# Attention trunk on one core: the values become the matmul's weights, pairs of query tiles move, 64-wide heads come out feature-major

## The chip, the cores and the metric

One core of a Trainium2 chip runs the whole program. The metric is the device time of one execution in microseconds (us). PE is TensorE, DVE is VectorE, ACT is ScalarE, POOL is GpSimd and SP is SyncE, which here only issues DMAs.

## What is computed

One layer over 1024 frames of width 1024, all in float32:

```
h = rmsnorm(x);  proj = h @ w_in
A: 4 heads, two maps of 64 each, values 128 wide, chunk-causal with a T5 bias; a = p0 - lam*p1; per-head rmsnorm
B: 8 heads of 64, band of own + 8 previous chunks (at most 5 tiles of 128 keys), relative bias
C: 8 heads of 64, causal, score + c_q - c_k from the forget gates
x += (sum_i sigmoid(gate_i) * (o_i @ w_br_i)) @ w_out
x += (silu(gt) * up) @ w_down;  out = rmsnorm(x)
```

## The kernel before

Every product that needs full accuracy is made of float32r halves: a high part (a rounded copy, made by ACT) and a low part (the rest, made by DVE or, for the weights, by POOL), and three passes (high x high, high x low, low x high). The program is four blocks, one after the other: norm, attention, merge, feed-forward. Each engine has its own instruction stream, in the order of the code, and waits on semaphores.

**Attention** is 12 units of two 64-wide maps or heads: units 0 to 3 are branch A (one head each), 4 to 7 branch B, 8 to 11 branch C. The first two branches are loops of two iterations over two units each; the units of C are written out. A unit has 16 steps s, and s stands for query tile i = s // 2 (128 queries) and map or head m = s % 2. Of each step:

- PE `score`: q tile is the weights, up to 8 key tiles move; the scores of map m land in two PSUM banks (m = 0: banks 0 and 1, m = 1: banks 2 and 3). In C one more matmul adds the causal mask on the diagonal tile.
- DVE `read_scores`: adds the bias, takes the row's extreme, writes `probs` (4 buffers). In C also `shift`.
- ACT `exp`, with the row's sum.
- PE `turn_probs`: transposes of the 128x128 tiles into banks 4 and 5, one chunk of up to 4 tiles in each. ACT `chunks_hi` and DVE `chunks_low` take each chunk out as `probs_t_hi` and `probs_t_lo`.
- PE `times_v`: for each key tile, the transposed probabilities are the weights and the values move, 128 columns in B and C (64 high, 64 low), 256 in A; once with the high and once with the low part. ACT `o_low_part` scales the half that came from the low values by 1/rowsum, DVE `o_out_part` scales the other, adds, and writes `heads` (2 buffers).

In A, `mix_maps` on DVE joins the two maps, and there is a transpose and a product only for every second step.

Between these PE makes the next unit's projection: 6 groups g of 512 frames (k, k, q, q, v, v), each in 4 **pieces** of 6 matmuls of 512 columns. `PIECES_AT[s]` says how many pieces step s has; 4 come ahead of step 0. A group's result is taken out of PSUM by `project_out` (ACT, two halves of 64 partitions) and `project_low` (DVE, two halves, for k and q) at the step that `EVAC_AT` names. In all units but 0 every group uses bank 6. The first piece of a group waits until the group before it is out:

```
if part == 0 and not (isinstance(unit, int) and unit == 0):
    pe.wait_ge(proj_out, 6 * unit + g)
```

PE's order in a step is: score(s+2), turn_probs(s), pieces, times_v(s-1). DVE's is: o_out_part(s-2), mix_maps (A), project_low, read_scores(s+2), chunks_low(s), and the reciprocal of the rowsum (B, C). ACT's is: o_low_part(s-2), project_out, chunks_hi(s), exp(s+2), and, at the steps of `SPLIT_AT`, the high part of a weight slab; POOL then makes its low part (`split_lo`, L559), three a unit. SP loads slabs and biases, shifts k between partitions, and stores `heads` to HBM token-major after each unit.

**Merge** goes over the branches in the order B, C, A, and in each over 8 feature tiles q: gate matmuls (2 halves x 24 matmuls of 512 columns), branch matmuls (24), sigmoid on ACT, products on DVE. The heads come back from HBM token-major, so each branch's heads are transposed on PE (L1203, 32 transposes of 128x128), B's all ahead of the first branch matmul, C's and A's one tile for each q through `heads_tile` (`stage`, L1141 for A, L1144 for C). The first gate (q = 0) is made in the last attention unit. Lines to know: L187 to L189 the three passes, L847/L848 score, L876 turn_probs, L895/L897 times_v, L694 to L703 project_low, L730 read_scores, L745 chunks_low, L773 o_out_part.

Of the kernel before, what the change touches and what calls it, by code (L numbers as in the profile page):

```python
# [26 lines left out]
F32 = mybir.dt.float32  # L27
# [5 lines left out]
P = 128  # L33
D = 1024
# [58 lines left out]
UNIT_TURNS = [len(turns_of(b)) for b in range(N_BRANCH)]  # L93
assert all(c % 2 == 0 for c in UNIT_CHUNKS)
V_CHUNKS = 2

# [7 lines left out]
PIECES_AT = [  # L104
# [20 lines left out]
assert all(PIECES_BEFORE + sum(pieces) == 6 * GROUP_PIECES for pieces in PIECES_AT)  # L125


def counts(b, it, du):

    unit = UPB * b + du + 2 * it  # L130
    local = du + 2 * it
    chunks = sum(UNIT_CHUNKS[:b]) * UPB + UNIT_CHUNKS[b] * local
    turns = sum(UNIT_TURNS[:b]) * UPB + UNIT_TURNS[b] * local
    return dict(unit=unit, local=local, step=STEPS * unit, chunks=chunks, turns=turns,
                banks=chunks + V_CHUNKS * unit)


def build(nc, x, norm_mix_g, w_in, b_forget, diff_lambda, diff_subln_g, t5_table, b_rel_table,
# [8 lines left out]
        heads=nc.dram_tensor("heads_scratch", (N_BRANCH, T, BR_W), F32, kind="Internal").ap(),  # L147
# [12 lines left out]

# [32 lines left out]
def block_norm(nc, ps, keep, scratch, x_tiles, norm_mix_g, w_in_k, b_forget, diff_lambda, diff_subln_g,  # L193
               t5_table, b_rel_table, norm_ffn_g, t5_onehot, rel_onehot):
    h_hi, h_lo, ident = keep["h_hi"], keep["h_lo"], keep["ident"]
    with ExitStack() as ctx:
        sb = lambda name, shape, dt=F32: ctx.enter_context(nc.sbuf_tensor(name, shape, dt))
        sem = lambda name: ctx.enter_context(nc.semaphore(name))
        x_all = sb("x_all", [P, TT, D])
# [7 lines left out]
        mask = sb("mask", [P, P])  # L207
# [50 lines left out]
        def _(pool):  # L258
            nc.gpsimd.memset(ident[:, :], 0.0).then_inc(made, 1)
            nc.gpsimd.memset(mask[:, :], 0.0).then_inc(made, 1)  # L260
            nc.gpsimd.memset(ones[:, :], 1.0).then_inc(made, 1)
            pool.wait_ge(made, 3)
# [3 lines left out]
            nc.gpsimd.affine_select(out=mask[:, :], in_=mask[:, :], compare_op=ALU.is_ge, fill=NEG,  # L266
# [1467 lines left out]
```

## Time and profile before

| | |
|---|---|
| median of 3 runs | 2133.78 us (2132.53 to 2134.18) |
| the profiled execution: its time, its span | 2137.23 us, 2135.5 us |
| granted TensorE clock, mean | 0.992 |
| PE busy | 2044.8 us, 96% of the span |
| PE weight loads busy | 1686.9 us, 79% |
| DVE, ACT, POOL busy | 942.5 (44%), 713.5 (33%), 97.6 us (5%) |
| DMA | 133.56 MB, 63 GB/s mean |

A matmul's duration in the trace reaches into the next one's (they are pipelined), so what a matmul costs is read from start to start. A unit of attention is bounded here by the first transpose of its values (L858): units begin at 87.2, 147.8, 208.4, 268.9 (A), 329.5, 396.2, 466.6, 533.3 (B), 600.0, 672.1, 744.1 and 813.1 us (C); the merge begins at 864.4.

### The profile page before, as it was taken

The page shows a single profiled execution, that of the slowest core. Times are in us where ns is not written, and L with a number is a line of the kernel's source. Part 1 is how long each engine was busy: PE and PEld are TensorE (multiplying, and loading weights), DVE is VectorE, ACT ScalarE, POOL GpSimd, SP SyncE. Part 2 cuts the span into 40 slices and gives each one's busy share as a digit, 9 for nine tenths or more (in the row PEclk, how much of TensorE's full clock was granted, in tenths as well). Part 3 has the DMA queues.
Part 4 walks back from the last instruction along what each step waited for, and adds up shares of the span by engine and source line. Part 5 has one row for each costly group of instructions (what it writes and reads, how often), then busy time and mean ns, then how long its engine had stood idle before and what let it go on. Part 6 is the DMA issues. An engine that isn't in the chain of part 4 may idle for free. (4 is left out here: it accounts for less than half of the span.)

```text
span 2135.5 us, 27733 instructions
## 1 busy us (share of the span) xinstructions
PE 2044.8 (96%) x10054; PEld 1686.9 (79%) x10054; DVE 942.5 (44%) x1894; ACT 713.5 (33%) x1374; POOL 97.6 (5%) x59
## 2 busy tenths in 40 slices
PE   7999999989999999899999999999999999999997
PEld 3787878878888888787787887778888888888886
DVE  4356665445555566322533236733432334323326
ACT  5355555545554555221332121321121111111122
POOL 1111111110010000000000000000000000000000
PEclk9999999999999999999999999999999999999999
DMA  7322122212222110312111113111121111211111
GB/s 220 106 63 79 40 71 73 72 34 55 65 79 65 50 51 31 113 44 84 44 44 45 44 49 148 40 39 41 59 59 49 31 43 54 59 49 37 43 50 79
DMA packets 153703, 133.56 MB, mean 63 GB/s; under 512 B 7701, under 2 KB 138901, under 8 KB 151305
## 3 DMA queue, kind: packets, MB, share of 16 engines
q1 hardware_dynamic: 150184, 132.16, 21.0%
q8 instruction: 55, 0.90, 0.2%
q10 hardware_dynamic: 3424, 0.17, 0.1%
q14 instruction: 40, 0.32, 0.1%
HBM read 109.17 MB, written 16.06 MB: 59 GB/s over the span
## 5 line engine op out<-in xcount | busy, mean ns | idle before, releaser
L187 PE MATMUL ps<-h_hi,w_hi 128*128 128x512 f32 x1664 | 670.4, 403 | 33.5 <-DVE k_stack L697 21.1
L189 PE MATMUL ps<-h_hi,w_lo 128*128 128x512 f32 x1664 | 658.1, 396 | 0.0
L188 PE MATMUL ps<-h_lo,w_hi 128*128 128x512 f32 x1664 | 657.5, 395 | 0.0
L187 PEld LDWEIGHTS ps<-h_hi,w_hi 128*128 128x128 f32 x1664 | 313.6, 188 | 111.1 <-DVE k_stack L697 26.3
L189 PEld LDWEIGHTS ps<-h_hi,w_lo 128*128 128x128 f32 x1664 | 313.2, 188 | 74.9
L188 PEld LDWEIGHTS ps<-h_lo,w_hi 128*128 128x128 f32 x1664 | 313.8, 189 | 68.4
L1482 DVE TENSOR_TENSOR residual<-residual,ps 128x512 f32<-128x512 f32 x240 | 162.5, 685 | 117.1 <-PE ps L189 112.1
L895 PE MATMUL ps<-v_split,probs_t_hi 128*128 128x128 f32 (+1 forms) x672 | 157.7, 273 | 3.7 <-DVE heads_out L773 3.5
L897 PE MATMUL ps<-v_split,probs_t_lo 128*128 128x128 f32 (+1 forms) x672 | 160.4, 277 | 0.0
L773 DVE SCALAR_TENSOR_TENSOR heads_out<-ps,rinv,o_low 128x64 f32<-128x64 f32 (+1 forms) x160 | 47.6, 297 | 245.3 <-ACT o_low L635 245.3
L730 DVE CUSTOM_DVE_ANT_0 probs<-ps,bias 128x640 f32<-128x640 f32 (+3 forms) x192 | 138.1, 721 | 23.9 <-PE ps L848 18.3
L895 PEld LDWEIGHTS ps<-v_split,probs_t_hi 128*128 128x128 f32 x672 | 128.1, 191 | 12.4 <-DVE heads_out L773 4.9
L897 PEld LDWEIGHTS ps<-v_split,probs_t_lo 128*128 128x128 f32 x672 | 128.4, 191 | 4.8
L1383 ACT ACTIVATE bias<-ps 128x512 f32<-128x512 f32 x44 | 26.1, 593 | 315.0 <-PE ps L189 314.9
L1473 DVE TENSOR_TENSOR w_lo<-w_raw,w_hi 128x1024 fp32r<-128x1024 f32 x46 | 56.4, 1225 | 161.6 <-ACT w_hi L1375 161.6
L617 ACT ACTIVATE probs<-probs,neg_max 128x640 f32<-128x640 f32 (+7 forms) x128 | 94.2, 736 | 99.9 <-DVE neg_max L730 99.4
L188 PE MATMUL ps<-w_down_lo,act_hi 128*128 128x512 f32 x320 | 124.5, 389 | 0.0
L187 PE MATMUL ps<-w_down_hi,act_hi 128*128 128x512 f32 x320 | 124.5, 389 | 0.0
L189 PE MATMUL ps<-w_down_hi,act_lo 128*128 128x512 f32 x320 | 124.5, 389 | 0.0
L745 DVE TENSOR_TENSOR probs_t_lo<-ps,probs_t_hi 128x384 fp32r<-128x384 f32 (+2 forms) x240 | 119.1, 524 | 9.9 <-ACT probs_t_hi L628 9.9
L559 POOL TENSOR_TENSOR w_lo<-w_raw,w_hi 128x1024 fp32r<-128x1024 f32 (+1 forms) x36 | 88.4, 2456 | 663.6 <-ACT w_hi L582 644.2
L628 ACT ACTIVATE probs_t_hi<-ps 128x384 fp32r<-128x384 f32 (+2 forms) x240 | 103.4, 466 | 25.9 <-PE ps L876 23.3
(191 smaller groups left out, 2462.1 us busy)
## 6 DMA issues: line engine op xcount, KB each, us to landing
w_raw<-in_w_in SPq DMA_DIRECT2D x60, 512.0 KB, 5.4
w_raw<-in_w_gate_up SPq DMA_DIRECT2D x44, 512.0 KB, 3.7
k_stack<-k_stack SPq DMA_DIRECT2D x24, 512.0 KB, 6.4
w_raw<-in_w_down SPq DMA_DIRECT2D x22, 512.0 KB, 3.5
heads_scratch<-heads_out SPq DMA_DIRECT2D x12, 512.0 KB, 3.2
bias<-heads_scratch SPq DMA_DIRECT2D x20, 256.0 KB, 4.7
x_all<-in_x SPq DMA_DIRECT2D x8, 512.0 KB, 10.1
bias<-bias_a_scratch SPq DMA_DIRECT2D x4, 1024.0 KB, 7.6
```

The costliest lines, as they stand in the source:

```text
L187: nc.tensor.matmul(out, w_hi, x_hi, start=first, stop=False)
L188: nc.tensor.matmul(out, w_hi, x_lo, start=False, stop=False)
L189: return nc.tensor.matmul(out, w_lo, x_hi, start=False, stop=last)
L559: nc.gpsimd.tensor_tensor(w_lo[part], w_raw[part], w_hi[part].bitcast(F32), ALU.subtract).then_inc(w_split, 1)
L617: nc.scalar.activation(probs[:, s % 4, 0:n], probs[:, s % 4, 0:n], ACT.Exp, scale=-1.0, bias=(shift if b == 2 else neg_max)[:, s % 4:s % 4 ...
L628: nc.scalar.activation(pt_hi[:, lc % 4, 0:size * P], turn_bank[lc % 2][:, 0:size * P], ACT.Copy).then_inc(turned_hi, 1)
L730: nc.vector.tensor_tensor_reduce(out=probs[:, s % 4, 0:n], in0=scores[m][:, 0:n], in1=window, scale=-1.0, scalar=3.0e38, op0=ALU.add, op1= ...
L745: nc.vector.tensor_tensor(pt_lo[:, lc % 4, 0:size * P], turn_bank[lc % 2][:, 0:size * P], pt_hi[:, lc % 4, 0:size * P].bitcast(F32), ALU.s ...
L895: nc.tensor.matmul(pv_bank[:, 0:width], pt_hi[:, lc % 4, x * P:(x + 1) * P], v, start=tile == 0, stop=False)
L897: last = nc.tensor.matmul(pv_bank[:, 0:width], pt_lo[:, lc % 4, x * P:(x + 1) * P], v, start=False, stop=tile == n - 1)
L1473: nc.vector.tensor_tensor(w_lo[kind], w_raw[:, raw, :], w_hi[kind].bitcast(F32), ALU.subtract).then_inc(w_split, 1)
L1482: nc.vector.tensor_tensor(res[:, t, cols], res[:, t, cols], bank(ps, 4 + o % 4), ALU.add).then_inc(added, 1)
```

## The change

In B and C the operands of `times_v` are swapped: the values (64 high and 64 low columns) are the weights, and the transposed probabilities of **two** query tiles, 256 columns, move. The result is feature-major: partitions 0 to 63 and 64 to 127 hold the products of the high and low values, 256 queries wide, in one half of bank 7. Key tiles that only one of the two query tiles sees move 128 columns.

- The steps of B and C are ordered so that a pair of tiles of one head is complete after two steps of each: `place_of` gives (0,0) (1,0) (0,1) (1,1) (2,0) ... for s = 0, 1, 2, 3, 4 ...; score banks go by s % 2.
- A query's rowsum now lies along the free axis of the product, so 1/rowsum is multiplied into the probabilities before they are transposed: `scale_probs`, a DVE TENSOR_SCALAR over the row for each of the 16 steps; `turn_probs` waits for it. Three buffers of probabilities in B and C.
- `o_low_part` and `o_out_part` become one ACT copy and one DVE add of 64x256 for each of 8 groups a unit.
- Scores of more than 4 key tiles are cut in two equal halves, not in 512 and the rest.
- Projection groups 0 and 1 use banks 3 and 1, the others bank 6; one schedule for all branches: pieces earlier, evacuations and weight splits at other steps. The wait quoted above stays.
- `heads` has one buffer, written 3 steps in after the store before it has landed; B's and C's heads are stored feature-major, one contiguous tile a unit. SP issues two slab loads ahead of the store.
- Merge: the heads of B and C are loaded feature-major and split straight from SBUF (`part_high` on ACT, DVE subtract), with no transposes and no staging; A keeps both, and is loaded by one DMA. The weights of gate q = 1 are loaded in the last unit, and its first half is computed ahead of the first branch matmul.
- The causal mask is made at the start of the attention block by POOL and DVE, not in the norm block; `ident` is read from `ident_r`.

```diff
+def place_of(branch, s):
+    if branch == 0:
+        return divmod(s, 2)
+    return 2 * (s // 4) + s % 2, s % 4 // 2
+def halves_of(n):
+    return (1, n * P) if n <= 4 else (2, n * P // 2)
-PIECES_AT = [ [0,2,2,0,2,2,0,2,2,0,2,2,0,1,2,0,1], ... ]
-EVAC_AT = [ {0: 0, 3: 1, 6: 2, 9: 3, 12: 4, 17: 5}, ... ]
-SPLIT_AT = [ {1: 1, 7: 2, 13: 3}, ... ]
+PIECES_AT = [2, 2, 2, 2, 0, 2, 2, 0, 2, 2, 0, 1, 1, 1, 1, 0, 0]
+EVAC_AT = {0: 0, 2: 1, 4: 2, 7: 3, 10: 4, 16: 5}
+SPLIT_AT = {0: 1, 5: 2, 10: 3}
...
-            return bank(ps, (0, 1, 2, 3, 5, 6)[g] if isinstance(unit, int) and unit == 0 else 6)
+            if isinstance(unit, int) and unit in (0, UNITS):
+                return bank(ps, (0, 1, 2, 3, 5, 6)[g] if unit == 0 else 6)
+            return bank(ps, (3, 1, 6, 6, 6, 6)[g])
...
+            def scale_probs(b, c, s):
+                turns = STEPS * (c["unit"] - UPB) + (s + 1)
+                row = probs_of(b, s)[:, 0:tiles_of(b, place_of(b, s)[0])[1] * P]
                 dve.wait_ge(probs_ready, c["step"] + (s + 1))
                 nc.vector.reciprocal(rinv[:, s % 4:s % 4 + 1], rowsum[:, s % 4:s % 4 + 1]).then_inc(rinv_ready, 1)
+                dve.wait_ge(rinv_ready, UPB * UNIT_OUTS + turns)
+                nc.vector.tensor_scalar(row, row, rinv[:, s % 4:s % 4 + 1], None, ALU.mult).then_inc(scaled, 1)
+            def o_out_bc(c, g):
+                near = slice((g % 2) * HD, (g % 2 + 1) * HD)
+                if g == 0:
+                    heads_room(c)
+                dve.wait_ge(o_low_ready, c["outs"] + (g + 1))
+                nc.vector.tensor_tensor(heads[near, g // 2 * 2 * P:(g // 2 + 1) * 2 * P], pv_half(g)[near, :],
+                                        o_low[near, :], ALU.add).then_inc(o_out, 1)
# DVE, one step
-                    if s - 2 in turns:
-                        o_out_part(b, c, s - 2)
+                    if b > 0 and s >= 3 and s % 2 == 1:
+                        o_out_bc(c, (s - 3) // 2)
...
                     if s + 2 < STEPS:
                         read_scores(b, c, s + 2)
+                    if b > 0 and s + 1 < STEPS:
+                        scale_probs(b, c, s + 1)
                     if s in turns:
                         chunks_low(b, c, s)
-                    if b > 0 and s < STEPS:
-                        invert(c, s)
# PE
+                    pe.wait_ge(scaled, STEPS * (c["unit"] - UPB) + (s + 1))
+            def times_v_bc(b, c, g):
+                i, m = 2 * (g // 2), g % 2
+                first, n = keys_of(b, g)
+                if g >= 2:
+                    pe.wait_ge(o_out, c["outs"] + (g - 1))
...
+                pe.wait_ge(turned_out, c["banks"] + (V_CHUNKS + chunks_through(b, 2 * g + 1)))
+                both = [k for k in range(n) if first + k <= i and first + k >= tiles_of(b, i + 1)[0]]
+                one = [k for k in range(n) if k not in both]
+                for k in both + one:
+                    lo = 0 if first + k <= i else P
+                    hi = 2 * P if first + k >= tiles_of(b, i + 1)[0] else P
+                    v = v_st[:, c["par"], first + k, m * P:(m + 1) * P]
+                    nc.tensor.matmul(pv_half(g)[:, lo:hi], v, ptb_hi[:, m, k, lo:hi], start=k == both[0], stop=False)
+                    last = nc.tensor.matmul(pv_half(g)[:, lo:hi], v, ptb_lo[:, m, k, lo:hi], start=False, stop=k == (both + one)[-1])
+                last.then_inc(pv_group, 1)
# merge, PE
             def tile_body(b, nt, q):
-                if b and isinstance(nt, int) and nt == 0:
-                    turn(b, TURNS - 1)
+                if b == N_BRANCH - 1 and isinstance(nt, int) and nt == 0:
+                    turn(TURNS - 1)
                 if isinstance(q, int) and q == 0:
                     pe.sem_inc(gate_ready, 2)
+                    gate(1, [0])
+                elif isinstance(q, int) and q == 1:
+                    gate(1, [1])
...
-                if isinstance(q, int) and q == 0:
-                    for t in range(TURNS):
-                        turn(0, t)
-                if b < N_BRANCH - 1 and not isinstance(nt, int):
-                    turn(b + 1, nt - 1)
+                if b == N_BRANCH - 2 and not (isinstance(nt, int) and nt == 0):
+                    turn(nt - 1)
```

## Rows read from the trace of the kernel before

**Rows 1.** Stretches of five units: us, busy PE PEld DVE ACT POOL, PEclk, DMA, GB/s.

```profile
87.20:147.80 60.60, 56.68 (x310) 48.01 (x309) 36.86 (x86) 30.86 (x67) 8.18 (x4) 1.00 0.18 46
...
329.50:396.20 66.70, 63.56 (x382) 54.89 (x381) 32.99 (x98) 35.10 (x87) 7.59 (x5) 1.00 0.22 59
396.20:466.60 70.40, 65.05 (x382) 56.09 (x381) 33.01 (x98) 35.10 (x87) 7.59 (x5) 0.98 0.25 71
...
672.10:744.10 72.00, 69.49 (x434) 61.07 (x433) 39.48 (x114) 37.81 (x87) 7.22 (x3) 1.00 0.21 60
...
813.10:864.40 51.30, 46.75 (x330) 42.52 (x330) 33.52 (x104) 30.81 (x77) 1.28 (x1) 1.00 0.10 32
```

**Rows 2.** Timeline of PE in an A unit: start, length, engine, line, out<-in.

```profile
104.69 0.40 PE L189 MATMUL ps<-h_hi,w_lo 128*128 128x512 f32 x1
104.92 0.28 PE L895 MATMUL ps<-v_split,probs_t_hi 128*128 128x256 f32 x1
105.04 0.28 PE L897 MATMUL ps<-v_split,probs_t_lo 128*128 128x256 f32 x1
```

**Rows 3.** Timeline of PE in a C unit, times_v.

```profile
700.94 0.27 PE L895 MATMUL ps<-v_split,probs_t_hi 128*128 128x128 f32 x1
701.05 0.27 PE L897 MATMUL ps<-v_split,probs_t_lo 128*128 128x128 f32 x1
```

**Rows 4.** Timeline, all engines: projection group 0 of unit 1 is taken out.

```profile
90.65 0.39 PE L189 MATMUL ps<-h_hi,w_lo 128*128 128x512 f32 x1
...
91.08 0.59 ACT L593 ACTIVATE k_stack<-ps 64x512 fp32r<-64x512 f32 x1 [2.13 <-PE ps L189]
...
91.70 0.68 DVE L694 TENSOR_TENSOR k_stack<-ps,k_stack 64x512 fp32r<-64x512 f32 x1 [1.15 <-ACT k_stack L593]
...
93.15 0.50 PE L187 MATMUL ps<-h_hi,w_hi 128*128 128x512 f32 x1 [1.51 <-DVE k_stack L697]
```

**Rows 5.** Timeline of DVE in a C unit: step with 6 key tiles.

```profile
709.05 0.96 DVE L730 CUSTOM_DVE_ANT_0 probs<-ps,bias 128x768 f32<-128x768 f32 x1
...
710.24 0.88 DVE L745 TENSOR_TENSOR probs_t_lo<-ps,probs_t_hi 128x384 fp32r<-128x384 f32 x2
711.03 0.15 DVE L750 RECIPROCAL rinv<-rowsum 128x1 f32<-128x1 f32 x1
```

**Rows 6.** Groups by line and shape: count, busy us, mean ns.

```profile
L351 DVE TENSOR_SCALAR x_all<-x_all,rstd 128x1024 f32<-128x1024 f32 x8 | 5.5, 749 | 0.1
...
L745 DVE TENSOR_TENSOR probs_t_lo<-ps,probs_t_hi 128x128 fp32r<-128x128 f32 x20 | 5.8, 288 | 3.4 <-ACT probs_t_hi L628 3.4
```

**Rows 7.** Timeline: a POOL split alone; DVE and POOL late in an A unit.

```profile
76.25 2.39 POOL L559 TENSOR_TENSOR w_lo<-w_raw,w_hi 128x1024 fp32r<-128x1024 f32 x1 [4.09 <-ACT w_hi L582]
...
137.60 1.28 DVE L762 SCALAR_TENSOR_TENSOR probs<-probs,ratio 128x1024 f32<-128x1024 f32 x1
...
138.15 2.99 POOL L559 TENSOR_TENSOR w_lo<-w_raw,w_hi 128x1024 fp32r<-128x1024 f32 x1 [18.96 <-ACT w_hi L582]
```

**Rows 8.** Timeline of PE: where the second iteration of B's loop begins.

```profile
461.75 0.47 PE L847 MATMUL ps<-k_stack,q_stack 128*128 128x128 f32 x1 [2.73 <-issue]
```

**Rows 9.** Timeline: end of attention and start of the merge.

```profile
862.47 0.27 PE L897 MATMUL ps<-v_split,probs_t_lo 128*128 128x128 f32 x1
...
864.46 3.56 PE L1203 MATMUL ps<-ident,bias 128*128 128x128 f32 x16 [1.71 <-SPq L1011]
...
879.45 0.50 PE L187 MATMUL ps<-h_hi,w_hi 128*128 128x512 f32 x1 [1.38 <-DVE w_lo L1102]
```

**Rows 10.** Timeline of PE in the merge, branches C and A.

```profile
1000.68 0.66 PE L1203 MATMUL ps<-ident,heads_tile 128*128 128x128 f32 x4 [1.29 <-DVE heads_tile L1144]
...
1146.25 0.66 PE L1203 MATMUL ps<-ident,heads_tile 128*128 128x128 f32 x4 [2.29 <-DVE heads_tile L1141]
```

**Rows 11.** Busy time and granted clock by stretch, behind two long waits.

```profile
462.00:466.00 4.00, 4.00 (x14) 3.34 (x15) 0.60 (x4) 0.88 (x4) 0.00 (x0) 0.62 1.00 313
...
1147.00:1151.00 4.00, 4.00 (x12) 3.15 (x11) 1.35 (x2) 1.15 (x2) 0.00 (x0) 0.59 0.15 45
```

More of the change, by code:

```diff
@@ L87, in chunks_through @@
 def chunks_through(branch, s):
-    return sum(len(chunks_of(branch, x // 2)) for x in turns_of(branch) if x <= s)
+    return sum(len(chunks_of(branch, place_of(branch, x)[0])) for x in turns_of(branch) if x <= s)
+def halves_of(n):
+    return (1, n * P) if n <= 4 else (2, n * P // 2)
 UNIT_CHUNKS = [chunks_through(b, STEPS - 1) for b in range(N_BRANCH)]
-UNIT_TURNS = [len(turns_of(b)) for b in range(N_BRANCH)]
+UNIT_OUTS = 8
 assert all(c % 2 == 0 for c in UNIT_CHUNKS)
@@ L124 @@
 assert sum(LAST_PIECES_AT) == 2 * GROUP_PIECES
-assert all(PIECES_BEFORE + sum(pieces) == 6 * GROUP_PIECES for pieces in PIECES_AT)
+assert PIECES_BEFORE + sum(PIECES_AT) == 6 * GROUP_PIECES
 def counts(b, it, du):
@@ L132, in counts @@
     chunks = sum(UNIT_CHUNKS[:b]) * UPB + UNIT_CHUNKS[b] * local
-    turns = sum(UNIT_TURNS[:b]) * UPB + UNIT_TURNS[b] * local
-    return dict(unit=unit, local=local, step=STEPS * unit, chunks=chunks, turns=turns,
+    return dict(unit=unit, local=local, step=STEPS * unit, chunks=chunks, outs=UNIT_OUTS * unit,
                 banks=chunks + V_CHUNKS * unit)
@@ new lines, in chunks_hi, with o_low_a, o_low_bc @@
+                    tile += size
+            def o_low_a(c, i):
+                act.wait_ge(pv_chunk, c["chunks"] + chunks_through(0, 2 * i + 1))
+                act.wait_ge(rinv_ready, c["outs"] + (i + 1))
+                nc.scalar.activation(o_low[:, i % 2 * P:(i % 2 + 1) * P], pv_bank[:, P:2 * P], ACT.Copy,
+                                     scale=rinv[:, 2 * (i % 2):2 * (i % 2) + 1]).then_inc(o_low_ready, 1)
+            def o_low_bc(c, g):
+                m = g % 2
+                near, far = slice(m * HD, (m + 1) * HD), slice((1 - m) * HD, (2 - m) * HD)
+                act.wait_ge(pv_group, GROUPS * (c["unit"] - UPB) + (g + 1))
+                nc.scalar.activation(o_low[near, :], pv_half(g)[far, :], ACT.Copy).then_inc(o_low_ready, 1)
@@ L924, in unit_body @@
                     if s + 2 < STEPS:
-                        score(b, c, s + 2)
+                        score(b, c, s + 2, last)
                     if s in turns:
@@ L982, in over_tiles @@
             body(0, KT * b)
+            if b == 0:
+                body(1, 1)
             end = KT - 1 if b == N_BRANCH - 1 else KT
-            with eng.Fori(1, end) as nt:
+            with eng.Fori(2 if b == 0 else 1, end) as nt:
                 body(nt, nt + KT * b)
@@ L987, in over_tiles, with flat @@
                 body(KT - 1, LAST)
+        def flat(parts):
+            return parts.rearrange("p k t -> p (k t)")
         def turn_view(t):
@@ L1204, in turn, with gate @@
                 last.then_inc(turned, 1)
+            def gate(q, halves=(0, 1)):
+                pe.wait_ge(g_split, q + 1)
+                for half in halves:
+                    cols = slice(half * HALF, (half + 1) * HALF)
+                    for k in range(KT):
+                        last = three_passes(nc, bank(ps, half), g_hi[:, k, :], g_lo[:, k, :],
+                                            h_hi[:, k, cols], h_lo[:, k, cols], k == 0, k == KT - 1)
+                    last.then_inc(gate_ready, 1)
@@ L1219, in tile_body @@
-                if isinstance(q, int) and q == 0:
-                    for t in range(TURNS):
-                        turn(0, t)
-                if b < N_BRANCH - 1 and not isinstance(nt, int):
-                    turn(b + 1, nt - 1)
+                    gate(1, [0])
+                elif isinstance(q, int) and q == 1:
+                    gate(1, [1])
+                else:
+                    gate(q)
+                if b == N_BRANCH - 2 and not (isinstance(nt, int) and nt == 0):
+                    turn(nt - 1)
```

426 lines of the change are left out of this document (233 added, 193 removed), and 6 rows, old and new, of tables (EVAC_AT, PIECES_AT).

## The prediction

> **What bounds the kernel now.** I read the page first: PE is busy for 96% of the span and no other engine for more than 44% (DVE), so time goes where PE's instructions and PE's waits go. The view by stretches then shows the units [rows 1]: an A unit lasts 60.6 us with PE busy 56.7, a B unit 66.7 with 63.6, a C unit 72.0 with 69.5. The reader is to see two things there. PE idles only 3.9, 3.1 and 2.5 us a unit, so there is little waiting to win; and DVE is busy for 37, 33 and 39.5 us of these, which a step-by-step dependence on DVE could turn into waits. Last the timeline of PE: start to start, a 512-column matmul costs 0.23 us, a 256-column one 0.12 [rows 2], a 128-column one with weights of its own 0.11 [rows 3]. So halving the columns below 256 saves nothing, and a product of 256 columns costs hardly more than one of 128.
>
> **What PE loses in work.** A C unit has 36 key tiles for each of 2 heads (1+...+8), two matmuls each: 144 x 0.111 = 16.0 us. After: pairs of query tiles see 2, 4, 6, 8 key tiles, of which one each is seen by one query tile alone: 32 x 2 x 0.12 + 8 x 2 x 0.111 = 9.4. A B unit goes from 60 tiles (13.3 us) to 24 of 256 and 12 of 128 columns (8.4). So C -6.5, B -4.9. The even cut of five-tile scores (512 + 128 becomes 320 + 320) gives another 0.3 in B and 0.1 in C by columns. Over 8 units -47 us, if PE never waited more than now.
>
> **What the new schedule makes PE wait for.** The wait in `piece` stays, so other banks don't help: group g+1 starts when group g is out, and that takes 2.27 us from the end of the pass (90.88 to 93.15: two ACT halves and two DVE halves) [rows 4]. I counted a unit through in the code's order with these pitches, PE against DVE; each wait below runs from the pitch's end, some 0.2 us more than the row's idle time (1.68 against 1.51 in rows 4), so the units above have 4.7, 4.1 and 3.3 of them.
>
> - A units, PE: before, two scores and a transpose stood between groups 0 and 1, and the count gives the 1.7 of rows 4; now one score does: 2.0. Group 2 follows group 1 in the very next step: 1.9 for 1.6. Group 3 waits 0.55 where it did not, group 4 0.85 for 0.55; the wait of the next unit's first group (0.8) goes, since group 5 ends earlier. The piece that lay between the last transposes and the last product is gone: ACT and DVE need a chunk first, 0.9. Together 6.2 for 4.7: +1.5 a unit, **A +6**.
> - B and C units, the same two waits: 1.9 and 1.75, for 1.6 before.
> - DVE in B and C: each step gets a TENSOR_SCALAR over the row. One of 1024 columns takes 0.75 us and a DVE instruction of 128 columns 0.29 [rows 6]; I take 0.28 + 0.067 per tile, and 0.2 for the reciprocal, whose end it waits for (its pitch alone is 0.07). 16 of them are about 10 us a unit, less 1.3 for half as many, wider output adds. DVE is then busy 43 to 48 us: not the bound by its sum. But it is in order: at s = 4 it stands waiting to take out group 2 and only then reads score 6 and scales step 5, which PE wants next. Group 2 out 2.27 after its end, read 0.8, scale 0.55: 3.6 us, in which PE has two scores, three transposes and a product, 1.8: **wait 1.9**. At s = 7 the chain is longer: product of group g = 2, ACT's copy, DVE's add, two halves of projection group 3, the read of six tiles (1.19 with `shift` [rows 5]), the scale 0.7: 5.35 us after the last piece, against 2.9 of PE work: **wait 2.5**. Later steps balance to within 0.6 in C.
> - The end of a unit: the product now waits for all of its chunks, with no piece ahead: 1.5.
> - What goes: all other waits of before, 2.5 in B and 1.7 in C (behind the first one).
>
> So B: 1.9 + 1.75 + 1.9 + 2.5 + 1.5 = 9.6 for 4.1, +5.5, less 5.2 of work: +0.3. C: 9.6 + 0.6 = 10.2 for 3.3, +6.9, less 6.6: +0.3.
>
> [...] The trace shows the two excluding each other: a POOL split alone takes 2.39 us, the one that began 0.55 us into a DVE operation on two SBUF rows took 2.99, longer by just what DVE had left [rows 7]. Whether DVE's new scaling waits for a split in the same way no row shows. Bounds: nothing, or a whole split for each of the three a unit, 7 us in B and C alike, 56 in all. Where the splits fall (s = 0, 5, 10) DVE has slack in the first two; at s = 10 it has not, and the scale is asked for 0.9 (B) or 0.3 (C) before the split ends. I take 1.2 and 0.3: B +1.5, C +0.6; four B units **+6**, three C units **+2**.
> [...]
>
> **The other terms.** The second iteration of B's loop begins with 2.73 us of PE idle on "issue" [rows 8], in which all engines stand, and then a halved clock: that unit lasts 70.4 for 66.7 [rows 1]. PE's body shrinks from 2 x 382 to 2 x 334 matmuls, near the 2 x 310 of A's loop, which shows no such wait; I take 2.5 of the 3.7: **-2.5** (0 to -3.7). The last unit has 8 pieces and few waits of projection: its work falls by 6.6; its start is serial through DVE (reads, values' low parts, scale) and costs 3 more: counted through 47.5 for 50.5, **-3**. POOL makes the mask ahead of the first split: **+0.5**.
>
> **Merge.** Before, the last product starts at 862.47 and the first gate after it at 879.45, so that gate q = 1 ends at 890.5 (48 x 0.23 on), 28.0 us later [rows 9]; in between stand 32 transposes and 24 matmuls. After: end of block 1.9 as now, ACT's and DVE's split of the gate weights 2.4, half a gate 5.5 with 1.8 for a clock that has fallen behind 4.3 us of waiting, 24 branch matmuls 5.5 (their heads are split meanwhile), the other half 5.5: 22.7. **-5.3.** C's 32 transposes (3.7 with their transitions) and their wait of 1.29 [rows 10] go: **-5.0.** A's are as before. Together -10.5; bounds -6 (if the 4 us of late heads' DMA shows) and -13.
>
> **Clock.** [...] I take one: **+1.5** (0, or +22 if each wait of 1.9 and 2.5 brings one).
>
> **Sum.** +6 (A) +6 (B) +2 (C) -2.5 -3 +0.5 -10.5 +1.5 = 0 on the profiled execution's own 2137.2 us (span 2135.5 and 1.7 around it). That execution is 3.4 above the median of the runs, so the median stays at 2134.
>
> **The rivals.**
> - *PE stays the bound* (faster). If DVE's order costs nothing at s = 5 and s = 8, because scores are read earlier than I count, 4.4 us a unit return in 7 units, and the clock's 1.5: -32, 2102. For it: DVE is busy only two thirds of a B unit. Against it: the two chains consist of instructions whose lengths are all in the rows. In part it can hold: at half, 2118.
> - *The port decides* (slower). A scale that meets a split stands up to 2.4 us, with read, chunk and PE's transposes behind it; at 1.2 us mean on three splits in 7 units that is 25 us, of which I have 6 in the sum; if two thirds reach PE, 17 for my 6: +11, 2145. From about 0.6 us more exposed a unit (4.3 over 7 units) it decides for slower. For it: the exclusion that rows 7 show. Against it: only one scale in five is due during a split.
> - *The clock falls often* (slower): in each of the 7 units with a wait of 2.5, +11 for my 1.5: 2144. With the port, 2154.
> - *The swap does nothing for PE*, the 256-column moves costing twice 0.11: then -47 is gone, 2178; rows 2 exclude it for the same shape, operands only exchanged.
>
> **How the numbers follow.** Forecast, gains eaten by waits, within 2123 to 2143: 0.5. PE the bound, wholly or in part: 0.22. Port: 0.15. Clock: 0.12. The last: 0.01. 2134 us is that of the likeliest; 8 in 10 reach from 2111 to 2149. A difference under 0.2% (4.3 us) is about what a measurement of this kernel can't tell from none; the forecast's own range lies on both sides of it. Faster: 0.16 of its 0.5 and 0.21 of PE's, 0.37. Slower: 0.09 of it, 0.23 of port and clock, and the last, 0.33. Same: 0.30.
>
> **What would show it.** L895/L897's successors in B and C: 304 pairs of matmuls for 528, 0.12 apart. PE's waits in B and C units: on DVE k_stack twice 1.5 to 1.8 us, on the DVE scaling at the 6th and 9th step, 2 to 2.5 us. PE idle 9 to 10 us in a B unit and a C unit, their lengths within 2 us of 66.7 and 72.0; A units 62. The gate of q = 1 ending 23 us behind the last product. A PEclk under 1.00 in some B and C units. A scale lasting much over 0.75 us, or DVE idle ahead of one during a POOL split, would show the port. Wrong it would be if B and C units come out 4 us shorter than now, or 4 longer.

## The result, and the profile after

The changed kernel takes 2156.2 us (median of 4 runs, 2153.4 to 2158.4) beside 2134.0 (4 runs, 2132.5 to 2135.0): 1.010 times the time before, 95% interval 1.009 to 1.012. It is slower by 22 us, where no change was forecast and 2149 us was the upper end of the range. The profiled execution has a span of 2154.3 us, 18.8 more than before.

The view by stretches shows five units that answer to [rows 1]:

```profile
86.00:150.30 64.30, 56.91 (x309) 47.94 (x308) 36.86 (x86) 31.04 (x67) 7.47 (x4) 1.00 0.19 48
150.30:217.70 67.40, 59.97 (x310) 50.59 (x308) 36.87 (x86) 32.26 (x68) 7.43 (x4) 0.95 0.23 64
...
350.70:419.20 68.50, 57.90 (x333) 49.40 (x332) 40.34 (x106) 34.79 (x79) 7.59 (x5) 1.00 0.22 58
...
710.40:789.40 79.00, 67.29 (x370) 57.83 (x369) 47.09 (x122) 37.52 (x79) 7.16 (x3) 0.94 0.19 54
864.40:916.50 52.10, 42.72 (x267) 36.81 (x267) 41.80 (x114) 29.40 (x68) 1.27 (x1) 0.97 0.08 31
```

An A unit, whose products are those of before, lasts 64.3 or 67.4 us for 60.6; the B unit 68.5 for 66.7; the C unit 79.0 for 72.0. PE has fewer instructions in B and C (333 and 370 for 382 and 434), and in the B unit PE is busy for 57.9 us instead of 63.6; what is lost is idle time and, in the units with a clock of 0.94 and 0.95, length of the instructions themselves.

The view of waits, PE in the attention block (what waited, for whom: us in total, times, longest). Before, the largest was `k_stack` with 21.1 us in 15 times, and nothing else was over 5.2:

```profile
PE ps L182 <- DVE k_stack L745: 37.4, 22, 1.9
PE ps L956 <- DVE probs_bc L813: 36.3, 21, 3.2
PE ps L956 <- DVE probs_tb_lo L801: 15.3, 17, 1.4
PE ps L993 <- DVE probs_tb_lo L801: 12.0, 8, 1.7
PE ps L972 <- DVE probs_ta_lo L798: 8.2, 8, 1.1
PE ps L182 <- DVE q_stack L751: 4.3, 8, 0.7
PE ps L956 <- DVE probs_a L825: 2.3, 4, 0.6
```

The first row is the evacuation wait, two in each of 11 units; the second the wait for a scaled row, 21 times in eight units. The next three are waits for low parts, mostly at the ends of units, where pieces used to lie.

What a wait brings beside its own length is in the timeline of PE in a C unit, step 6 to step 9:

```profile
655.36 0.22 PE L930 MATMUL ps<-causal_r,ident_r 128*128 128x128 f32 x1
657.46 0.66 PE L956 MATMUL ps<-ident_r,probs_bc 128*128 128x128 f32 x4 [1.88 <-DVE probs_bc L813]
657.87 0.48 PE L182 MATMUL ps<-h_hi,w_hi 128*128 128x512 f32 x1
658.19 0.39 PE L183 MATMUL ps<-h_lo,w_hi 128*128 128x512 f32 x1
658.42 0.53 PE L184 MATMUL ps<-h_hi,w_lo 128*128 128x512 f32 x1
658.75 0.63 PE L182 MATMUL ps<-h_hi,w_hi 128*128 128x512 f32 x1
659.18 0.63 PE L183 MATMUL ps<-h_lo,w_hi 128*128 128x512 f32 x1
...
661.31 0.63 PE L182 MATMUL ps<-h_hi,w_hi 128*128 128x512 f32 x1
661.74 0.48 PE L183 MATMUL ps<-h_lo,w_hi 128*128 128x512 f32 x1
662.06 0.40 PE L184 MATMUL ps<-h_hi,w_lo 128*128 128x512 f32 x1
...
671.57 0.55 PE L956 MATMUL ps<-ident_r,probs_bc 128*128 128x128 f32 x3 [2.58 <-DVE probs_bc L813]
```

Behind 1.88 us of idle time the passes start 0.43 us apart instead of 0.23, from 658.75 to 661.74, and the granted clock of 657 to 661 is 0.69; from 658.9 to 661.5 it is 0.50. So it stands at half for some eight passes, 1.6 us lost. In attention the trace holds 18 such drops, before 1: five in A, four in B, eight in the three C units of this length, one in the last.

The start of the merge (timeline of PE, answering to [rows 9]; last product, first gate, first pass behind the gate):

```profile
916.54 0.28 PE L994 MATMUL ps<-probs_tb_lo,v_split 128*128 128x128 f32 x1
921.51 0.80 PE L182 MATMUL ps<-h_hi,w_hi 128*128 128x512 f32 x1 [4.70 <-DVE w_lo L1223]
...
939.49 0.39 PE L182 MATMUL ps<-o_hi,w_hi 128*128 128x512 f32 x1
```

The gate of q = 1 ends 22.95 us behind the last product (939.49 less 916.54); 28.2 before, where the first instruction behind it starts at 890.70.

By stages the spans differ so. Attention, from the first transpose of values to the last product: 775.3 before, 830.5 after. Merge, to the first addition of the residual: 426.5 and 406.6. Output projection and norm: 94.0 and 90.9. The rest, the feed-forward block, whose code is the same: 752.5 and 740.3. The last number had no place in the forecast, and the first experiments are about it.

### The profile page after: what moved, and what is told of

It is laid out like the page before. It is cut to its first block and busy times, and to the rows that moved or that the text cites. A ratio compares the mean times of both kernels' runs of the same rounds, so it can differ in the third digit from the quotient of the medians.

```text
span 2154.3 us, 26265 instructions
## 1 busy us (share of the span) xinstructions
PE 1988.8 (92%) x9542; PEld 1647.9 (76%) x9542; DVE 999.7 (46%) x1950; ACT 710.8 (33%) x1310; POOL 94.5 (4%) x59
## 5 line engine op out<-in xcount | busy, mean ns | idle before, releaser
L182 PE MATMUL ps<-h_hi,w_hi 128*128 128x512 f32 x1664 | 674.3, 405 | 51.2 <-DVE k_stack L745 37.4
L184 PE MATMUL ps<-h_hi,w_lo 128*128 128x512 f32 x1664 | 658.9, 396 | 0.0
L184 PEld LDWEIGHTS ps<-h_hi,w_lo 128*128 128x128 f32 x1664 | 318.7, 192 | 69.5
L183 PEld LDWEIGHTS ps<-h_lo,w_hi 128*128 128x128 f32 x1664 | 319.6, 192 | 62.0
L956 PE MATMUL ps<-ident_r,probs_bc 128*128 128x128 f32 x528 | 85.2, 285 | 51.9 <-DVE probs_bc L813 36.3
L780 DVE CUSTOM_DVE_ANT_0 probs_bc<-ps,bias 128x640 f32<-128x640 f32 (+7 forms) x128 | 90.0, 703 | 53.5 <-PE ps L930 24.2
L956 PEld LDWEIGHTS ps<-ident_r,probs_bc 128*128 128x128 f32 x528 | 60.1, 143 | 66.4 <-DVE probs_bc L813 40.8
L1607 DVE TENSOR_TENSOR bias<-ps,bias 128x512 f32<-128x512 f32 x44 | 30.4, 691 | 167.2 <-PE ps L184 167.2
L665 ACT ACTIVATE probs_tb_hi<-ps 128x384 fp32r<-128x384 f32 (+2 forms) x192 | 82.6, 463 | 74.0 <-PE ps L956 72.6
L927 PE MATMUL ps<-k_stack,q_stack 128*128 128x320 f32 (+5 forms) x288 | 98.3, 345 | 0.0
L928 PE MATMUL ps<-k_stack,q_stack 128*128 128x320 f32 (+5 forms) x288 | 95.5, 335 | 0.0
L1504 ACT ACTIVATE act_hi<-bias 128x512 fp32r<-128x512 f32 x44 | 27.8, 632 | 202.9 <-DVE bias L1607 202.9
L801 DVE TENSOR_TENSOR probs_tb_lo<-ps,probs_tb_hi 128x384 fp32r<-128x384 f32 (+2 forms) x192 | 93.8, 516 | 2.1 <-ACT probs_tb_hi L665 1.7
```

The lines of the kernel that those rows point to most:

```text
L182: nc.tensor.matmul(out, w_hi, x_hi, start=first, stop=False)
L183: nc.tensor.matmul(out, w_hi, x_lo, start=False, stop=False)
L184: return nc.tensor.matmul(out, w_lo, x_hi, start=False, stop=last)
L665: nc.scalar.activation(turned_place(ptb_hi, b, i, m, tile, size), turn_bank[lc % 2][:, 0:size * P].rearrange("p (t q) -> p t q", q=P), ACT ...
L780: nc.vector.tensor_tensor_reduce(out=row_view(probs_of(b, s)[:, 0:n * P], n), in0=scores_view(s, n), in1=row_view(window, n), scale=-1.0, ...
L801: nc.vector.tensor_tensor(turned_place(ptb_lo, b, i, m, tile, size), turn_bank[lc % 2][:, 0:size * P].rearrange("p (t q) -> p t q", q=P), ...
```

## The experiments

Twelve kernels, three groups. Where a median is compared, that of the kernel before is 2135 to 2137 us beside these runs, and that of the changed kernel 2156.2. The changed kernel was measured once, beside 2134.0, so differences from it carry up to 3 us of drift.

**1. Where do buffers lie?** The passes over `h_hi` and `h_lo` had been 233 ns apart before and were 227 after. The change dropped one buffer and put the small ones ahead of `h_hi`. (No trace shows an address. What each run differs in is the order and the sizes in which its kernel declares the buffers.)

*place*, the kernel before with that order:

```diff
         keep = dict(
-            h_hi=sb("h_hi", [P, KT, T], F32R), h_lo=sb("h_lo", [P, KT, T], F32R),
-            ident=sb("ident", [P, P]), ident_r=sb("ident_r", [P, P], F32R),
-            causal_r=sb("causal_r", [P, P], F32R),
+            ident_r=sb("ident_r", [P, P], F32R),
...
+            h_hi=sb("h_hi", [P, KT, T], F32R), h_lo=sb("h_lo", [P, KT, T], F32R),
+            ident=sb("ident", [P, P]), causal_r=sb("causal_r", [P, P], F32R),
```

> [...] No instruction differs but in its addresses. Theory (the address of the moving operand sets the pitch of a 512-column matmul): the 4,944 passes over h_hi and h_lo go from a mean of 233.2 ns to 227.4, the up-projection's stage is 12 us shorter, and the whole 29 us: 2105 us. Rival (the shorter pitch after came from something else in the changed program): no change, 2134.

Measured: 2109.7 us, 0.987 of before (0.986 to 0.989). *unplace*, the changed kernel with `h_hi` and `h_lo` moved ahead of the small buffers:

> [...] Address theory: 2156 + 29 = 2185 us, with the pitch at 233 ns again, and a little less in attention, where part of it is hidden by waits: 2178 to 2185. Rival: 2156.

Measured: 2182.2 us, 1.022 of before (1.020 to 1.023). So 26 to 27 us of the changed kernel's time are a gift of the order of the buffers, in either kernel, and the change itself costs 46.

What about the order counts? *pad128* puts 128 bytes (`pad=sb("pad", [P, 32])`) ahead of `h_hi` in the kernel before:

> [...] If the address is not it at all: 2137.

Measured: 2136.5 us, 1.000 (0.999 to 1.001). No pitch changed: 233.2 ns over `h_hi` and `h_lo` in the feed-forward block, 226.9 in the last projection. So the same 128 bytes ahead of the moving operand and of the weights do nothing, to the passes at 233 ns or to those at 227. What is left is the distance between the two. By the author's estimate (worked out in the last section) it is an odd multiple of 128 bytes where passes are 233 ns apart and an even one where they are 227 apart. *padw* has the same line ahead of `bias`, so that 128 bytes more stand between `h_lo` and the weights; *place_padw* is *place* with that line:

> [...] In the slow programs so far (before, unplace, pad128) the moving operand and the weights of a pass lie an odd multiple of 128 bytes apart, in the fast ones (place, the changed kernel, and act_hi with w_down_hi everywhere) an even one. Distance theory: the pitch goes to 227 ns, 2137 - 27 = 2110 us. [...]

> [...] Distance theory: the pitch goes back to 233 ns, 2137 us. Rival (h_hi's address alone): 2110, as place.

Measured: padw 2112.3 us, 0.990 (0.988 to 0.992); place_padw 2137.4, 1.001 (1.000 to 1.002). What stands between the two decides, and not the place of one of them alone: with `h_hi` ahead of the small buffers and with `h_hi` behind them, the same 128 bytes ahead of the weights turn 233.2 ns into 226.7 and 226.7 into 233.2. From the timelines of PE in the feed-forward block, first and last pass of a row of passes: before, 50 passes apart,

```profile
1499.80 0.40 PE L187 MATMUL ps<-h_hi,w_hi 128*128 128x512 f32 x1
...
1511.46 0.40 PE L189 MATMUL ps<-h_hi,w_lo 128*128 128x512 f32 x1
```

padw, 39 passes apart,

```profile
1499.83 0.39 PE L190 MATMUL ps<-h_hi,w_lo 128*128 128x512 f32 x1
...
1508.67 0.39 PE L190 MATMUL ps<-h_hi,w_lo 128*128 128x512 f32 x1
```

and place_padw, 50 passes apart:

```profile
1499.69 0.40 PE L188 MATMUL ps<-h_hi,w_hi 128*128 128x512 f32 x1
...
1511.36 0.40 PE L190 MATMUL ps<-h_hi,w_lo 128*128 128x512 f32 x1
```

11.66 / 50 = 0.2332, 8.84 / 39 = 0.2267, 11.67 / 50 = 0.2334 us. A matmul's own length hardly shows it (0.39 or 0.40); only start to start does.

**2. Which waits, and whose?** *sched* gives the changed kernel the three schedules of before:

```diff
-PIECES_AT = [2, 2, 2, 2, 0, 2, 2, 0, 2, 2, 0, 1, 1, 1, 1, 0, 0]
-EVAC_AT = {0: 0, 2: 1, 4: 2, 7: 3, 10: 4, 16: 5}
-SPLIT_AT = {0: 1, 5: 2, 10: 3}
+PIECES_AT = [0, 2, 2, 0, 2, 2, 0, 2, 2, 0, 2, 2, 0, 1, 2, 0, 1]
+EVAC_AT = {0: 0, 3: 1, 6: 2, 9: 3, 12: 4, 17: 5}
+SPLIT_AT = {1: 1, 7: 2, 13: 3}
```

> The changed kernel with the schedule of before: the steps at which pieces are computed, taken out and split are before's three lists; banks, scaling and the wider products stay. Theory (the bunched pieces cause the evacuation waits, and the halved clock follows them): A units return from 66 to 61.5 us, B and C units lose 3 and 5 us, the clock drops fewer than 8 times in attention for 18: 2156 - 18 - 12 - 15 = 2111 us. Rival (the scaling on DVE causes the waits of B and C): only A returns, 2138 us, and B and C units keep 70 and 78 us.

Measured: 2124.2 us, 0.995 of before (0.993 to 0.996), 32 below the changed kernel. All four A units last 60.0 or 60.1 us, as in *place*; B falls by 2.4 us in all, the three C units by 7.8. Of the 36.6 us between the two profiled executions, 24.5, two thirds, are thus A's, where the product was not changed at all; both theories had A returning, while B and C gave back less than the first had, and nine drops are left in attention where it had fewer than eight. The wait for scaled rows has even grown:

```profile
PE ps L956 <- DVE probs_bc L813: 49.5, 26, 2.9
PE ps L956 <- DVE probs_tb_lo L801: 27.6, 17, 2.7
PE ps L182 <- DVE k_stack L745: 11.7, 8, 1.5
```

*noscale* cuts the scaling's length, not its place in DVE's order (rows beyond their first 8 columns stay unscaled):

```diff
-                nc.vector.tensor_scalar(row, row, rinv[:, s % 4:s % 4 + 1], None, ALU.mult).then_inc(scaled, 1)
+                nc.vector.tensor_scalar(row[:, 0:8], row[:, 0:8], rinv[:, s % 4:s % 4 + 1], None, ALU.mult).then_inc(scaled, 1)
```

> The changed kernel with the scaling of a row cut to its first 8 columns, so DVE keeps the instruction, its waits and its signal, and loses its length (the rows stay unscaled). Theory of the forecast (the scale is the last of DVE's chain ahead of PE's transposes): the waits of 1.9 and 2.5 us at the 6th and 9th step fall to 1.3 and 1.7, the end of the unit by 0.7, 1.9 us a unit and with them half of the drops of the clock: 2156 - 13 - 8 = 2135. Rival (evacuations and reads of DVE alone make these waits): 2150 or above.

Measured: 2134.3 us, 22 below the changed kernel, as expected in sum (2135), though not in its parts. The wait for the scaled row goes from 36.3 us only to 31.0; at the 9th step of a C unit it is 2.26 us for 2.58, shorter by just what that scaling lost (0.55 to 0.23). The rest of the 22 is in low-part waits (15.3 to 8.6) and six drops of the clock fewer. So these waits are made by what DVE has queued ahead of the scaling more than by the scaling. (Scalings that meet a split on POOL did not get shorter, up to 1.3 us for 8 columns; more on this at the end.) The timeline of DVE in the changed kernel, ahead of the 2.58 above, shows that queue:

```profile
667.54 0.42 DVE L846 TENSOR_TENSOR heads_out<-ps,o_low 64x256 f32<-64x256 f32 x1 [2.20 <-ACT o_low L682]
668.16 0.68 DVE L748 SCALAR_TENSOR_TENSOR q_stack<-ps,q_stack 64x512 fp32r<-64x512 f32 x1 [0.20 <-ACT q_stack L630]
668.86 0.69 DVE L751 SCALAR_TENSOR_TENSOR q_stack<-ps,q_stack 64x512 fp32r<-64x512 f32 x1
669.58 0.96 DVE L780 CUSTOM_DVE_ANT_0 probs_bc<-ps,bias 128x768 f32<-128x768 f32 x1
...
670.96 0.55 DVE L813 TENSOR_SCALAR probs_bc<-probs_bc,rinv 128x640 f32<-128x640 f32 x1
```

*loose* takes the evacuation wait away where banks allow it:

```diff
-                    pe.wait_ge(proj_out, 6 * unit + g)
+                    pe.wait_ge(proj_out, 6 * unit + (g if g > 2 else 0))
```

> The changed kernel with the wait ahead of a projection group cut to what its bank needs: groups 1 and 2 stand in banks of their own, so they wait only for group 5 of the unit before, as group 0 does, and no longer for groups 0 and 1. Theory (these two waits, 2.0 and 1.9 us in every unit, and the halved clock behind them are what A's units lost): A units go from 66.2 to 61 us (-4 of waits, -1.5 of clock), B and C units lose half of that, since there the row's scaling waits next: 2156 - 20 - 2.5 x 7 = 2118. Rival (groups leave no faster than DVE and ACT take them out, so group 3 inherits the waits): 2145 or above.

Measured: 2100.7 us, 0.984 of before (0.982 to 0.985), 55 below the changed kernel, a far larger gain than in either expectation. The list of PE's waits is that of the changed kernel with its first row gone (scaled rows 36.1, low parts 15.4, 12.0 and 8.1): 37.4 us of waits went and next to nothing took their place (1.1 us for a weight split), and drops in attention fell from 18 to 7. 37.4 + 11 x 1.6 = 55. A units last 60.4 to 60.7.

*fill* leaves the waits and covers part of them with matmuls whose product is thrown away:

```diff
+                if part == 0 and g in (1, 2) and not (isinstance(unit, int) and unit in (0, UNITS)):
+                    for _ in range(4):
+                        nc.tensor.matmul(proj_bank(unit, g), keep["ident_r"][:, :], h_hi[:, 0, 0:HALF], start=True, stop=True)
                 if part == 0 and not (isinstance(unit, int) and unit == 0):
...
+                    if s in (5, 8):
+                        pe.wait_ge(turned_out, c["banks"] + (V_CHUNKS + done - 1))
+                        for _ in range(4):
+                            nc.tensor.matmul(turn_bank[done % 2], keep["ident_r"][:, :], h_hi[:, 0, 0:HALF], start=True, stop=True)
                     pe.wait_ge(scaled, STEPS * (c["unit"] - UPB) + (s + 1))
```

> The changed kernel with four 512-column matmuls of no use (their product is overwritten) ahead of each of four waits: those for groups 1 and 2 in every unit, and those for the scaled row at the 6th and 9th step of B and C. They last 0.9 us, less than each wait. Theory (a good part of the loss is the halved clock, 18 drops between 86 and 917 us at some 1.7 us each): at least 14 of the 18 go, the waits themselves stay: 2156 - 24 = 2132. Rival (the drops lie mostly in other waits, or filling only adds work): 2156 to 2165.

Measured: 2133.0 us, 0.999 of before (0.998 to 1.000), 23 below the changed kernel, with 3 drops in attention for 18. 23.2 / 15 = 1.5 us a drop. A kernel that computes 152 matmuls more is faster by 23 us; what waits for DVE is otherwise as it was (low parts 15.2, 12.0 and 8.2 us), so this is the price of the clock.

**3. Can both be had?** *sched_late* is *sched* with PE's pieces ahead of its transposes in B and C:

```diff
+                    if b > 0:
+                        next_pieces(pieces_at[s])
                     if s in turns:
                         turn_probs(b, c, s)
-                    next_pieces(pieces_at[s])
+                    if b == 0:
+                        next_pieces(pieces_at[s])
```

> The run sched (changed kernel, schedule of before) with PE's order changed in B and C alone: in each step the pieces of projection come ahead of the transposes of the row. Its turns wait 3.0, 1.3, 2.8 and 1.6 us for the scaled row. Theory (DVE finishes the scaling late in every step by less than two pieces last, 2.8 us, so PE has work to put in front): B units from 69.4 to 66, C units from 75.4 to 71: 2124 - 14 - 13 = 2097. Rival (DVE's order of work is the bound and what PE does first only moves the wait to the next score or group): 2120 to 2130.

Measured: 2083.0 us, 0.975 of before (0.974 to 0.977), 41 below *sched* and 14 below what the first theory gave. B units last 64.4 (one 65.9), C units 68.8 (the last of the three 65.8). PE's largest waits are now these; the wait for scaled rows has gone from 49.5 to 4.1, and a part has come back ahead of the groups:

```profile
PE ps L182 <- DVE k_stack L745: 35.3, 22, 1.9
PE ps L182 <- DVE q_stack L751: 7.9, 11, 1.2
...
PE ps L956 <- DVE probs_bc L813: 4.1, 3, 2.6
```

*best* adds the looser wait to it (`0 if banks_apart else g`, with `banks_apart` for g up to 2, but not in the unit that computes the first gate, whose groups share a bank):

> Changed kernel with the schedule of before, pieces ahead of the transposes in B and C (both as in sched_late), and the wait ahead of groups 1 and 2 cut to what their banks need (as in loose, though not in the unit that computes the first gate). If the two cures act on different waits: A units from 60.0 to 57, B and C units 2 less: 2083 - 12 - 14 = 2057. If what loose removed is only the wait that the bunched schedule made: 2083.

Measured: 2048.5 us, 0.959 of before (0.957 to 0.960), 9 better than expected. The two cures act on different waits: an A unit lasts 57.9 us, a B unit 61.0 to 61.2, a C unit 65.9 (the third 63.0), and one drop is left in attention. By stretches, units 1, 5 and 9:

```profile
144.50:202.40 57.90, 56.12 (x310) 48.01 (x309) 36.78 (x86) 31.80 (x68) 8.16 (x4) 1.00 0.27 75
...
379.20:440.30 61.10, 57.82 (x334) 49.19 (x333) 38.75 (x103) 32.56 (x75) 7.62 (x5) 1.00 0.24 64
...
628.50:694.40 65.90, 62.93 (x370) 54.19 (x369) 49.01 (x122) 36.55 (x79) 7.25 (x3) 1.00 0.23 65
```

*best_dve* also turns DVE's order round in B and C:

```diff
+                    if b > 0 and s + 1 < STEPS:
+                        scale_probs(b, c, s + 1)
                     if project and s in EVAC_AT:
                         project_low(c["unit"] + 1, EVAC_AT[s], 1 - du)
                     if s + 2 < STEPS:
                         read_scores(b, c, s + 2)
-                    if b > 0 and s + 1 < STEPS:
-                        scale_probs(b, c, s + 1)
```

> The run best with DVE's order changed in B and C: the scaling of a row stands ahead of a group's low part and of the next read of scores. If DVE's order is what still delays PE's transposes there: 1 to 1.5 us a unit less, -10 in all. If the read of scores is by now the later of the two: 0 to +10.

Measured: 2060.4 us, 12 above *best*: B and C units 0.4 to 0.8 longer, the last unit 55.6 for 50.5. What comes late with the scaling first is the low part of a projection group: the wait on `q_stack` grows from 1.22 to 1.85 us in a B unit and from 0.49 to 1.37 in a C unit. That is not the read of scores that the second theory named. In the last unit, which takes no group out, the waits for low parts of probabilities grow, most of them 1.2 to 1.7 us each; whether a late read of scores is behind these was not tested.

## Why the prediction was wrong, point by point

The view by stretches of whole branches (A, B, the three C units of full length) of *unplace*, which has the pitch of before (233 ns) and is the fair partner for a forecast that took it as given; its last unit is 52.0:

```profile
86.90:354.30 267.40, 238.53 (x1234) 199.48 (x1233) 147.69 (x344) 125.59 (x269) 29.98 (x17) 0.96 0.22 57
354.30:633.30 279.00, 236.81 (x1332) 200.39 (x1331) 161.34 (x426) 139.01 (x316) 29.94 (x18) 0.99 0.21 57
633.30:867.40 234.10, 198.92 (x1093) 170.16 (x1092) 140.50 (x360) 111.77 (x233) 21.49 (x9) 0.94 0.18 51
```

and of the kernel before:

```profile
87.20:329.50 242.30, 226.58 (x1234) 191.99 (x1233) 147.42 (x344) 124.79 (x269) 32.92 (x17) 1.00 0.23 62
329.50:600.00 270.50, 255.85 (x1523) 220.94 (x1522) 132.41 (x394) 140.50 (x348) 29.95 (x18) 0.99 0.22 59
600.00:813.10 213.10, 205.64 (x1285) 180.88 (x1283) 117.66 (x338) 112.47 (x257) 21.66 (x9) 1.00 0.21 58
```

| term of the sum | forecast | measured, pitch as before |
|---|---|---|
| A's four units | +6 | +25.1 |
| B's four units, with the loop's stall | +3.5 | +8.5 |
| three C units | +2 | +21.0 |
| last unit | -3 | +2.6 |
| mask, start | +0.5 | -0.3 |
| merge | -10.5 | -10.2 |
| clock | +1.5 | 16 drops more (17 for 1), in the rows above |
| output projection | none | -1.3 |
| order of the buffers | none | -26.6 |

The rows come to +45 without the last and +19 with it, which is the difference of the spans.

- **Two steps failed, about equally.** With the pitch of before, attention grew by 57 us (25.1 + 8.5 + 21.0 + 2.6), where the forecast had 8.5 for the new waits less the work saved, and 1.5 for the clock.
- **The clock: "I take one".** No run shows the term, one drop of 1.5 us for all new waits. The rows of before have the granted clock at 0.62 and 0.59 of 4 us behind waits of 2.73 and 2.29 us [rows 8, 10, 11], and at 1.00 in the unit with the wait of 1.51 [rows 1, 4]; they give it for no length between. What the runs showed in its place is 17 drops more in the changed kernel and 16 more in *unplace*, at 1.5 us each by *fill* some 25 us for 1.5. The forecast's own upper bound, "+22 if each wait of 1.9 and 2.5 brings one", is about what came. The waits were there in the forecast; what they would do to the clock was its author's guess. Of the 18 drops of the changed kernel ten stand behind idle times of 1.7 to 1.9 us, four of them in A units, seven behind 2.4 to 3.2, and one behind 1.05. The length does not decide alone: unit 0 has the same waits as unit 1 and no drop, and the first B unit has waits of 1.80 and 2.46 and none. What else decides stays open. The rival "the clock falls often" named the right cause, with one drop in each of 7 units and none in A, and so less than half the price.
- **The size of the waits.** The other 32 us stand against 8.5: the waits at the end of A, B and C units and at the start of the last unit were counted too short, as the next points show.
- **PE's work**, -5.2 in B and -6.6 in C: right. It is best read where the clock keeps still: from *place* to *best*, PE's busy time falls from 254.4 to 231.5 us in B and from 204.5 to 185.9 in three C units, 5.7 and 6.2 a unit (5.3 in B without the one drop that *place* has there). "The swap does nothing" is out.
- **A, +1.5 a unit:** a unit without a drop is 64.3 - 60.0 = 4.3 longer than in *place*. The two evacuation waits (1.87 and 1.76) and the smaller ones came as counted. What was short is the tail, 0.9 for three waits of 0.94, 0.57 and 1.05 in these rows of unit 2; with the 0.2 that the forecast adds to each wait that is some 2.2 of the 2.8 us missing, and the rest stays open:

```profile
273.56 0.38 PE L972 MATMUL ps<-v_split,probs_ta_hi 128*128 128x256 f32 x1 [0.94 <-DVE probs_ta_lo L798]
...
276.06 1.09 PE L956 MATMUL ps<-ident_r,probs_a 128*128 128x128 f32 x8 [0.57 <-DVE probs_a L825]
278.20 0.39 PE L972 MATMUL ps<-v_split,probs_ta_hi 128*128 128x256 f32 x1 [1.05 <-DVE probs_ta_lo L798]
```

  The last pieces hid not one chunk's conversion but the ends of two steps. And "the wait in `piece` stays, so other banks don't help" was true and was the costliest line of the kernel: *loose* shows 55 us behind it.
- **B and C, the waits for the scaled row, 1.9 and 2.5:** measured 1.88 and 2.58 in the C unit above, right. "Later steps within 0.6 in C" was not: low parts at the last steps cost 1.37, 0.84 and 1.66 us in unit 9, for 1.5 + 0.6. A B unit without a drop came out at 68.5 us in the changed kernel and at 68.9 and 69.2 in *unplace*, for a forecast of 68.5 (66.7 + 0.3 + 1.5). That it fits is luck in part: of the port's 1.5 at most 0.6 can have reached PE, and the low parts at its end cost 3.0 (1.31, 0.35 and 1.34) for 1.5. A C unit came out at 79.0, 6.1 above its forecast (72.0 + 0.3 + 0.6): three drops and 1.5 us of waits.
- **PE stays the bound** is refuted for this kernel. It came true in *best*, by other edits than the rival had in mind: PE is busy there for 96% of the span.
- **The port:** no run shows a port. What they show is that a scaling on DVE that meets a split on POOL is held up by it (1.17 us for 0.49), as the forecast assumed; the cost was set too high. Two rows of DVE and one of POOL:

```profile
378.76 2.40 POOL L589 TENSOR_TENSOR w_lo<-w_raw,w_hi 128x1024 fp32r<-128x1024 f32 x1 [17.37 <-ACT w_hi L616]
```

```profile
380.27 1.17 DVE L813 TENSOR_SCALAR probs_bc<-probs_bc,rinv 128x512 f32<-128x512 f32 x1
...
393.62 0.55 DVE L813 TENSOR_SCALAR probs_bc<-probs_bc,rinv 128x640 f32<-128x640 f32 x1
```

  A scaling of 640 columns alone takes 0.55 us, one of 512 that meets a split 1.17; nine of 128 are longer by more than 0.6 and add some 6 us to DVE in all: two in each B unit, one in the last unit, none in the three C units between. The first of a B unit does not reach PE: DVE waits 1.62 us for ACT soon after it (383.52). The second stands ahead of the low part for which PE waits 1.31, so at most 0.6 a unit, 2.5 in all, reached PE. The forecast had 8 on PE.
- **B's stall on "issue"** (-2.5): gone, PE has no such wait left in attention.
- **The last unit:** -3 was too hopeful. It is 2.6 longer than before: PE idles 9.4 us in it for 3.1, of which one wait for a scaled row at its start is 3.2, and a drop follows. It lasts 50.5 us even in *best*.
- **Merge:** -10.5 forecast, -10.2 measured. Behind the wait of 4.70 ahead of the gate the granted clock is 0.51 from 921.3 to 924.7, 1.7 us lost for the 1.8 of the forecast. The gate's end is 22.95 us behind the last product for 22.7; with the pitch of before, which the forecast knew, it is 24.55, so this part was somewhat short and the rest of the merge made it up.
- **Order of the buffers:** no step of the forecast looked at it. It hid 27 of 46 us: without it the forecast would have been twice as far off.

## What to carry to other kernels

Price each new wait on TensorE with what it does to the clock: here 37 us of waits cost 55, and covering part of the waits with useless matmuls won 23. When banks are dealt out anew, loosen the waits to what the banks need in the same edit, and put work that depends on nothing ahead of work that waits for a long chain. Before comparing two versions, look at the start-to-start pitch of an untouched stage: if it differs, as here (226.7 for 233.2 ns in the feed-forward block), hold the order of the buffers fixed, which was worth 27 us in *place* and 26 in *unplace*.

## What the runs showed of the hardware

Passes of 512 fp32r columns over `h_hi` and `h_lo` in the feed-forward block start 226.7 ns apart in the changed kernel, *place*, *padw* and *best*, and 233.1 to 233.2 on average (nearly all of them 229 to 238) before and in *pad128*, *place_padw* and *unplace*. The output projection, where `act_hi` moves and `h_hi` is the weights, falls into the same two groups: 226.8 to 227.0 ns in the first four, 233.3 before and 232.3 to 232.4 in the other three. The last projection, where `w_down_hi` moves and `act_hi` is the weights, has 226.7 to 226.9 in all eight. 2.8% of such a pitch is 27 us here. 128 bytes between `h_lo` and the weights change it, in one direction (*padw*) and in the other (*place_padw*), and 128 bytes ahead of both do not (*pad128*).

An estimate of the distance from `h_hi` to `w_hi` within the partition can be worked out from the sizes that the kernels of the runs declare, if buffers lie one behind the other in the order of the code and the two of 4 bytes take 32 each, both of which are assumptions and shown by no trace: 751 x 128 bytes before and in *pad128*, 743 in *unplace* and 745 in *place_padw*, with the pitch of 233 ns; 736 in the changed kernel, 744 in *place* and 752 in *padw*, with that of 227. That the one goes with odd multiples and the other with even ones rests on this estimate. Only one size of padding was tried, and why the distance matters stays open.

A one-row scaling on DVE that starts up to 2.1 us into a split on POOL (2.4 us, the smaller one 1.27) ends behind the split's end, the direction that no row of before showed. It is clearest in *noscale*, where a scaling of 8 columns lasts 0.23 us alone:

```profile
402.12 2.40 POOL L589 TENSOR_TENSOR w_lo<-w_raw,w_hi 128x1024 fp32r<-128x1024 f32 x1 [19.20 <-ACT w_hi L616]
```

```profile
403.69 0.86 DVE L813 TENSOR_SCALAR probs_bc<-probs_bc,rinv 128x8 f32<-128x8 f32 x1
```

Sixteen such scalings start 0.06 to 2.1 us into a split there, and every one ends 0.03 us behind the split's end. In the changed kernel those of 512 columns end 0.28 us behind it and those of 640 columns 0.35, which is about 0.067 us for each 128 columns. Alone the three lengths last 0.23, 0.49 and 0.55 us, so of each some 0.20 us lies within the split and the rest behind it. The row of 512 columns above takes 1.17 us, and 0.49 where no split runs. Three scalings of 8 columns that start 2.27 us into a split of 2.40 are not held up: they take 0.23 us and end 0.10 behind it.
